# A diffusion backbone step: the block inverses of RWKV's pairs on four quarters of TensorE, in seven levels

## The reference, cut to what matters

```
def _rwkv_direction(r, w, k, v, a, b, s0):
    def step(state, inp):
        r_t, w_t, k_t, v_t, a_t, b_t = inp
        sa = jnp.einsum('bhvk,bhk->bhv', state, a_t)
        state = (state * w_t[:, :, None, :] + sa[..., None] * b_t[:, :, None, :]
                 + v_t[..., None] * k_t[:, :, None, :])
        return state, jnp.einsum('bhvk,bhk->bhv', state, r_t)
```

## Time and profile before

| | |
|---|---|
| timed runs, median | 2022.66 us |
| the profiled execution's own time | 2029.15 us |
| its span in the profile | 2027.2 us |
| mean granted TensorE clock | 0.96 |
| TensorE matmul busy | 1910.2 us (94%) |
| TensorE weight load busy | 1748.5 us (86%) |
| VectorE busy | 1095.8 us (54%) |
| ScalarE busy | 739.1 us (36%) |
| instructions | 38671 |

### The profile page before, as it was taken

The page is one execution under the profiler, slowest core; times in us unless marked ns, Lnnn a source line. Parts: engine busy times, 40 slices in busy tenths (PEclk is TensorE's granted clock), DMA queues, the critical chain, the costliest instruction groups (busy, mean ns, idle before and its releaser), DMA issues. The chain is left out here.

```text
span 2027.2 us, 38671 instructions
## 1 busy us (share of the span) xinstructions
PE 1910.2 (94%) x16360; PEld 1748.5 (86%) x16360; DVE 1095.8 (54%) x1845; ACT 739.1 (36%) x1108; POOL 33.2 (2%) x62
## 2 busy tenths in 40 slices
PE   5999999998888989999999999999978898999997
PEld 2888999995665879999999999999747497999997
DVE  3544444865537466554455554476564756655533
ACT  3333333435224244333343333344441424433322
POOL 0000000000001000000000000000000100000000
PEclk9999999998789999999999999999979798999999
DMA  7766233423446233333343333442240401333332
GB/s 271 263 224 222 90 129 137 158 101 113 142 129 212 85 109 125 124 124 113 127 145 124 124 118 114 138 169 90 87 148 4 159 13 66 125 124 124 105 128 89
DMA packets 73192, 263.25 MB, mean 130 GB/s; under 512 B 9696, under 2 KB 10848, under 8 KB 56928
## 3 DMA queue, kind: packets, MB, share of 16 engines
q1 hardware_dynamic: 73056, 261.27, 37.9%
HBM read 259.08 MB, written 2.16 MB: 129 GB/s over the span
## 5 line engine op out<-in xcount | busy, mean ns | idle before, releaser
L157 PE MATMUL ps<-h_head,w_head 128*128 128x386 f32 x1824 | 624.0, 342 | 9.2 <-DVEq L243 4.1
L157 PE MATMUL ps<-h_head,w_rest 128*128 128x386 f32 x1824 | 619.3, 340 | 0.0
L157 PE MATMUL ps<-h_rest,w_head 128*128 128x386 f32 x1824 | 617.3, 338 | 0.0
L219 ACT ACTIVATE w_head<-w_raw 128x2048 fp32r<-128x2048 f32 (+1 forms) x176 | 303.0, 1721 | 609.2 <-PE ps L157 598.9
L222 DVE TENSOR_TENSOR w_rest<-w_raw,w_head 128x2048 fp32r<-128x2048 f32 (+1 forms) x176 | 360.7, 2049 | 204.4 <-ACT w_head L219 204.3
L157 PEld LDWEIGHTS ps<-h_head,w_head 128*128 128x128 f32 x1824 | 345.9, 190 | 28.6 <-issue 18.8
L157 PEld LDWEIGHTS ps<-h_head,w_rest 128*128 128x128 f32 x1824 | 345.8, 190 | 0.0
L157 PEld LDWEIGHTS ps<-h_rest,w_head 128*128 128x128 f32 x1824 | 343.0, 188 | 0.2
L157 PE MATMUL ps<-gu_head,w_head 128*128 128x384 f32 x832 | 279.9, 336 | 11.4 <-DVE gu_rest L813 11.4
L157 PE MATMUL ps<-gu_rest,w_head 128*128 128x384 f32 x832 | 279.4, 336 | 0.0
L157 PE MATMUL ps<-gu_head,w_rest 128*128 128x384 f32 x832 | 279.3, 336 | 0.0
(11 more groups left out here) (294 smaller groups left out, 1798.1 us busy)
## 6 DMA issues: line engine op xcount, KB each, us to landing
w_raw<-in_w_in SPq DMA_DIRECT2D x88, 1024.0 KB, 4.8
w_raw<-in_w_out SPq DMA_DIRECT2D x64, 704.0 KB, 4.0
w_raw<-in_ada_w SPq DMA_DIRECT2D x41, 1024.0 KB, 6.2
ada_raw<-in_ada_w SPq DMA_DIRECT2D x31, 1024.0 KB, 6.4
w_raw<-in_mix_in SPq DMA_DIRECT2D x26, 1024.0 KB, 4.9
w_raw<-in_mix_out SPq DMA_DIRECT2D x8, 1024.0 KB, 5.0
hyena_const<-in_hconst SPq DMA_DIRECT2D x2, 1792.0 KB, 9.6
x<-in_x_in SPq DMA_DIRECT2D x1, 1536.0 KB, 12.2
```

The source lines that it names most:

```text
L157: return nc.tensor.matmul(out, lhsT, rhs, start=start, stop=stop)
L219: return nc.scalar.activation(self.HI[src], self.RAW[src], ACT.Copy)
```

## The change

The two directions now go through the inverse together. A new helper `crossed` issues the products of both: direction 0 on the two quarters as before, direction 1 with rows 0 to 63 of the array against columns 64 to 127 and the other way round, into a second PSUM bank. Direction 1's result therefore lands with its heads swapped, and the next product swaps them back. `straight` issues both directions on the old two quarters, where no swap is wanted (`pe_t`, `pe_y`). The first squares (`pe_s1`) keep the old two quarters too.

The running sums are replaced by products: T = I + D is multiplied by I + D^2 (`J2`), I + D^4 (`J4`) and I + D^8 (`J8`), and Y = (I + EX^2)(I + EX) Q. There are seven levels: `s1`; `d4`, `t1`, `x4`; `t2`, `x8`; `t`; `q`, `ex`; `gm`, `y1`, `ex2`; `y`. A pair issues 336 matmuls for its inverses, where it issued 288. Most copies out of PSUM now take both directions at once, 128x768 over two neighbouring banks; X^4 and EX are read twice by VectorE, once with the identity added and once plain.

The pairs share bank 3 in place of bank 6, since the two banks of a copy must be neighbours; GLA and pair B move to banks 4, 5, 6. B may write bank 3 when A's `y1` is copied. All four hand-written queues are reordered: the `ada_products` of the second set are issued during A's inverse, and in `two_pairs_stage` B's inverse is laced with A's recurrence.

```diff
--- before.py
+++ after.py
@@ -1340,13 +1340,12 @@
-                                " ".join(f"s{i}_{z}" for i in ("1", "2") for z in z2) + " s2q_0 s2q_1 s3_0 s3q_0 s3_1 s3q_1 " +
-                                " ".join(f"s{i}_{z}" for i in ("4", "5", "6", "7", "8", "9") for z in z2) + " " +
+                                "s1_0 s1_1 d4 t1 x4 t2 x8 t q ex gm y1 ex2 y " +
...
-                                " ".join(f"s{i}_{z}" for i in (1, 2, 3, 5, 6) for z in z2) + " u0 u1 u2 u3 o sq std")
+                                "d2_0 d2_1 d4 t1 t_0 q gm y1 y_1 u0 u1 u2 u3 o sq std")
...
-                                " ".join(f"s{i}_{z}" for i in ("1", "2q", "3q", "4", "7", "8", "9") for z in z2) + " " +
+                                "x2_0 x2_1 j2_0 j2_1 j4 x4 t2 j8 t_1 je ex jg y_0 " +
...
-                self.D, self.D2, self.D4, self.Y, self.ET = (by_chunk(b) for b in (self.SIG, self.E2, self.E3, self.CUM, self.E1))
-                self.GS, self.D8, self.EX = self.D4, self.D2, self.D
+                self.D, self.D2, self.J2, self.J4, self.ET = (by_chunk(b) for b in (self.SIG, self.E2, self.E3, self.CUM, self.E1))
+                self.X, self.T = (self.XQ[:, :, :, x, :] for x in range(2))
+                self.D4, self.X4, self.J8 = self.D, self.D2, self.X
+                self.INV, self.Q, self.EX, self.JE, self.G = self.J2, self.T, self.D, self.J4, self.X
+                self.Y1, self.JG, self.Y = self.D2, self.ET, self.J4
...
-            def each(self, b, lhsT, rhs):
-
-                for c, e in PROBS:
-                    last = mm(bank(b, TOK)[half(e), c * C:c * C + C], lhsT(c, e), rhs(c, e))
+            def crossed(self, ba, bb, lhsT, rhs):
+                for c in range(NCH):
+                    for h in range(2):
+                        mm(bank(ba, TOK)[half(h), c * C:c * C + C], lhsT[half(h), 0, c, :], rhs[half(h), 0, c, :])
+                    for h in range(2):
+                        last = mm(bank(bb, TOK)[half(1 - h), c * C:c * C + C], lhsT[half(h), 1, c, :], rhs[half(h), 1, c, :])
                 return last
...
+            def straight(self, ba, bb, lhsT, rhs):
+
+                for z, b in enumerate((ba, bb)):
+                    for c in range(NCH):
+                        for h in range(2):
+                            last = mm(bank(b, TOK)[half(h), c * C:c * C + C], lhsT[half(h), z, c, :], rhs[half(h), z, c, :])
+                return last
+
+            def even(self):
+                return (self.b0, self.b1) if self.b3 > self.b2 else (self.b1, self.b2)
+
+            def odd(self):
+                return (self.b2, self.b3) if self.b3 > self.b2 else (self.b3, self.b0)
+
+            def both(self, banks):
+                ba, bb = banks
+                assert bb == ba + 1
+                return PS[:, ba * 512:bb * 512 + 512].rearrange("p (z x) -> p z x", x=512)[:, :, 0:TOK].rearrange("p z (c t) -> p z c t", t=C)
+
+            def one_of(self, banks, z):
+                return bank(banks[z], TOK).rearrange("p (c t) -> p c t", t=C)
...
-            def pe_s2(self, pe, z):
-                ba, _ = self.pair_banks(z)
-                self.after_act(pe, f"s1_{z}")
-                self.after_dve(pe, f"s1_{z}")
-                self.pe_step(self.each(ba, self.power(z), self.of(self.D2, z)), f"s2_{z}")
...
-            def pe_s789(self, pe, i, z):
-                ba, _ = self.pair_banks(z)
-                if i == 7:
-                    self.after_act(pe, f"s6_{z}")
-                else:
-                    self.after_dve(pe, f"s{i - 1}_{z}")
-                self.pe_step(self.each(ba, self.of(self.EX, z), self.q(z) if i == 7 else self.of(self.Y, z)), f"s{i}_{z}")
+                ba, bb = self.even()[z], self.odd()[z]
+                for b, lhsT, rhs in ((ba, self.X, self.D), (bb, self.D, self.X)):
+                    for c in range(NCH):
+                        for h in range(2):
+                            last = mm(bank(b, TOK)[half(h), c * C:c * C + C], lhsT[half(h), z, c, :], rhs[half(h), z, c, :])
+                self.pe_step(last, f"s1_{z}")
+
+            def pe_d4(self, pe):
+                self.after_act(pe, "d2_1")
+                self.after_dve(pe, "x2_1")
+                self.pe_step(self.crossed(*self.even(), self.X, self.D2), "d4")
+
+            def pe_t1(self, pe):
+                self.after_dve(pe, "j2_1")
+                self.after_pool(pe, "q1")
+                self.pe_step(self.crossed(*self.odd(), self.J2, self.T), "t1")
+
+            def pe_x4(self, pe):
+                self.after_act(pe, "d4")
+                self.pe_step(self.crossed(*self.even(), self.D2, self.X), "x4")
+
+            def pe_t2(self, pe):
+                self.after_dve(pe, "j4")
+                self.after_act(pe, "t1")
+                self.pe_step(self.crossed(*self.odd(), self.J4, self.T), "t2")
+
+            def pe_x8(self, pe):
+                self.after_dve(pe, "x4")
+                self.pe_step(self.crossed(*self.even(), self.D4, self.X4), "x8")
+
+            def pe_t(self, pe):
+                self.after_dve(pe, "j8")
+                self.pe_step(self.straight(*self.odd(), self.J8, self.T), "t")
...
+            def pe_ex(self, pe):
+                self.after_act(pe, "t_0")
+                self.after_dve(pe, "t_1")
+                self.pe_step(self.crossed(*self.odd(), self.ET, self.INV), "ex")
+
+            def pe_g(self, pe):
+                self.after_act(pe, "q")
+                self.pe_step(self.crossed(*self.even(), self.INV, self.ET), "gm")
+
+            def pe_y1(self, pe):
+                self.after_act(pe, "q")
+                self.after_dve(pe, "ex")
+                self.pe_step(self.crossed(*self.odd(), self.JE, self.Q), "y1")
+
+            def pe_ex2(self, pe):
+                self.after_act(pe, "gm")
+                self.after_dve(pe, "ex")
+                self.pe_step(self.crossed(*self.even(), self.G, self.EX), "ex2")
+
+            def pe_y(self, pe):
+                self.after_dve(pe, "jg")
+                self.after_act(pe, "y1")
+                self.pe_step(self.straight(*self.even(), self.JG, self.Y1), "y")
 
             def pe_x(self, pe, t):
                 if t == 0:
-                    self.after_dve(pe, "s9_1")
+                    self.after_dve(pe, "y_0")
+                    self.after_act(pe, "y_1")
...
+            def act_both(self, act, name, out, banks):
+                self.after_pe(act, name)
+                self.act_step(nc.scalar.activation(out, self.both(banks), ACT.Copy), name)
+
+            def act_d4(self, act):
+                self.after_pool(act, "q1")
+                self.act_both(act, "d4", self.D4, self.even())
...
+            def dve_one_plus(self, dve, product, out, banks, name):
+                self.after_pe(dve, product)
+                ones = cst("istack").unsqueeze(1).unsqueeze(1).to_broadcast([128, 2, NCH, C])
+                self.tt(out, self.both(banks), ones, ALU.add, name)
+
+            def dve_one_plus_x4(self, dve):
+                self.dve_one_plus(dve, "x4", self.J4, self.even(), "j4")
+
+            def dve_x4(self, dve):
+                self.after_pe(dve, "x4")
+                self.dve_step(nc.vector.tensor_copy(self.X4, self.both(self.even())), "x4")
...
-                A = Pair(scope, SEMS[0:5], lay, 0, (0, 1, 2), 6, PR, TG, AL, MO)
-                G = Gla(scope, SEMS[5:10], lay, (3, 4, 5), P, MO)
+                A = Pair(scope, SEMS[0:5], lay, 0, (0, 1, 2), 3, PR, TG, AL, MO)
+                G = Gla(scope, SEMS[5:10], lay, (4, 5, 6), P, MO)
...
-                A = Pair(scope, SEMS[0:5], lay, 1, (0, 1, 2), 6, PR, TG, AL, MO)
-                B = Pair(scope, SEMS[5:10], lay, 2, (3, 4, 5), 6, PR, TG, AL, MO, (A.act_done, A.AC["s6_1"]))
+                A = Pair(scope, SEMS[0:5], lay, 1, (0, 1, 2), 3, PR, TG, AL, MO)
+                B = Pair(scope, SEMS[5:10], lay, 2, (4, 5, 6), 3, PR, TG, AL, MO, (A.act_done, A.AC["y1"]))
```

476 lines of the change are left out of this document (214 added, 262 removed).

## The result

The changed kernel takes 2045.1 us (median of 4 runs, 2041.07 to 2048.98) against 2022.84 us for the kernel before beside it. The ratio is 1.0102, 95% interval 1.0085 to 1.0118: about 1% slower, where 0.5% faster was forecast. The medians differ by 22.3 us.

A forecast was written before the change was run, and what follows sets the result against it. It took the inverse as bound by TensorE and the recurrence by round trips of x and u through VectorE. Four stage gains summed to -9.5 us off the median 2022.66: 2013 us, eight-in-ten range 2003 to 2030.

The forecast's parts named there:

- The question that it took for the risk: Crossed steps of the inverse: whether four quarters run side by side; 0.70 us for 24 matmuls, up to 1.40 without overlap.
- A crossed step takes 0.70 to 0.80 us.: Inverse, timeline after: the successor of a crossed step of 48 records starts 0.70 to 0.80 us later.
- the slower rival: Ten crossed steps of each inverse: four quarters are no faster than two, 1.40 us a step, 2042 us; 14%.
- GLA stage, second layer, -3.2: Second layer's GLA stage: inverse ends sooner, part is lost again before the second x; -3.2 us.
- GLA stage, first layer, -2.2: First layer's GLA stage: five `ada_products` cover most waits in the inverse, the second round loses that cover; -2.2 us.
- what else moves I cost at nothing: ... SP's loads only start sooner: Everything else that moves, including modulation weights, pool's T = I + D and SP's loads: priced at nothing.
- Two-pair stages, -3.3 and -0.8: Two-pair stages: A's first x comes much earlier and the stage ends sooner; -3.3 us first layer, -0.8 us second.
- A's norm is now out of the way and the end loses its doubled copies: Second layer's two-pair stage, after B's first x: a shorter end, last output at 69.4 us, before 70.2.
- The clock: Mixer stages: TensorE is busy 77% at a granted 1.00 in the recurrence, and no stretch much emptier was expected.
- The sign of a wrong mechanism: The four stages: the mechanism is wrong if their granted clock falls below that of the windows before.
- The sum: All four stages together: -3.2 - 2.2 - 0.8 - 3.3 = -9.5 us.

The follow-up runs named there:

- e1: Kernel before plus a block of crossed, straight and load-accompanied crossed steps that wait for nothing; a long-running crossed step took 1.37 us.
- e3: Changed kernel with every crossed step made straight (two quarters instead of four); ratio 1.0143 to the kernel before.
- e2: Changed kernel with the second sets' modulation weight loads cut to one eighth in the first layer; ratio 1.0029 to the kernel before.
- e13: Kernel before with its old inverse, but the second layer's two-pair stage in the changed kernel's order; ratio 1.0030, stage 76.5 us.
- e14: Kernel before with the new inverse in the second layer's two-pair stage, B on its own banks, both recurrences in step; ratio 1.0003, stage 69.3 us.
- e5: Kernel before with the change in the GLA stages of both layers only; ratio 1.0006.
- e6: Kernel before with the change in the two-pair stages of both layers only; ratio 1.0074.
- e9: Kernel before with the new inverse in the second layer's two-pair stage, B on its own banks, its recurrence one round behind; ratio 1.0039, stage 78.8 us.
- e7: Kernel before with the change in the GLA stages only, the second set's products left in their old places; ratio 1.0002.
- e12: Kernel before with the change in the second layer's GLA stage alone, a repeat with more rounds; ratio 0.9986.

## Why the prediction was wrong

The question that it took for the risk, whether four quarters overlap, was answered rightly. What decided the time, how fast instructions reach TensorE, was not in it, and the order that lets A go first was priced too low.

- *A crossed step takes 0.70 to 0.80 us.* Right in the trace (0.75), and the copies (0.81, 0.95) to the hundredth. But 0.70 us holds only while instructions lie ready. In the long run it is 1.37 us (e1). That the slower rival (2042 us) comes near the measured 2045.1 is luck: its cause, quarters that don't overlap, is refuted by the 0.75, and with steps that really take 1.40 us the kernel comes to 1.0143 (e3), some 2052 us. The trace's 48 records in 0.70 us are 15 ns each, where the Trainium skill's "TensorE: Matmul & The Clock Gate", section "Wait — 56ns, not 53.3ns?", has a floor of 25; over a whole stream they are 28.5 ns (3.65 us for 128).
- *GLA stage, second layer, -3.2.* Measured -3.1, but by two misses that cancel: A's x stands at 31.3 us instead of the 29.6 worked out (1.4 us of stops ahead of it), and behind the second x (38.0) the recurrence gained 1.0 us where I had given it nothing.
- *GLA stage, first layer, -2.2.* Measured +7.8. The step that failed is "what else moves I cost at nothing: ... SP's loads only start sooner". The loads, started sooner by the products in the inverse, fell on the instruction fetches, and a step priced at 0.70 us took its instructions faster than they came: 6.5 us of stops (2.3 are left in e2 without the loads), and some 3 us of half clock behind them (0.6 and 0.7 us in the two rows behind the stop at 555.88, 0.25 for `t`, 0.8 for `y` at 576.57, 0.6 for the two products behind it). Together 9.5 of the 10.0 us between forecast and result; e2's stage is 6.5 us shorter.
- *Two-pair stages, -3.3 and -0.8.* Measured +7.0 and +5.0. Stops are 5.7 and 2.0 of that. A's x came as worked out in the second layer (25.3 against 25.6), B's at 46.5 against 43.8. The step that failed is "A's norm is now out of the way and the end loses its doubled copies": from B's first x to the end of the last output I gave 25.6 us, it took 28.8, because B runs its round trips alone and the granted clock goes to 0.50, TensorE's 1.2 GHz. e13 prices the order at 6.9 us without any new level; in the changed kernel the levels gave about 2 of it back (74.7 against 76.5), and without the order they give nothing (e14). In the first layer A's x came at 32.2 instead of 27.9, and B's at 53.2, 7.9 us later than before (45.3), while the part from there on took 28.9 against 29.8: there the whole loss stands ahead of B's first x. I had counted what ends A's inverse sooner, and put B's delay against it too low.
- *The clock.* The sign of a wrong mechanism came: the granted clock fell in three of four stages (0.92, 0.89, 0.90 in the windows above). Their busy shares are 84, 79 and 78%, no lower than the 77% that I had gone by, so the share of a whole stretch did not tell it. The half clock stands behind the long stop and in the lone tail, where TensorE is busy for 5.75 of 11.70 us (726.33 to 738.03). The idle 3.71 us with a lower clock behind it stood in the earlier trace rows as a warning.
- *The sum.* GLA stages +4.7, two-pair stages +12.1, elsewhere +1.2 in the trace. e5 and e6 put the larger part on the two-pair stages too: 0.06% (-0.15 to 0.26) and 0.74% (0.52 to 0.96).

What could have been read before: TensorE's 863 matmul and 863 weight-load records in 31.31 us are 55 a us, and the change asks for 96 instructions in 0.70 us in its steps. That is a question to ask, though no row of before showed the limit. At the 70 a us of e1 or the 76 of e9, the 336 matmuls of a pair, 1344 instructions, take 18 to 19 us, an estimate: no less than the 18.1 us of the inverse before.

Stage times of single executions scatter: with the same stage code the second layer's two-pair stage took 74.7 and 76.0 us in two kernels and 77.3 in e2, with 2.0, 5.1 and 3.7 us of stops, and I can't say why e2's is longest. How much of the two-pair stages' loss is supply, and how much order, is therefore known to 2 or 3 us only. That a fetch waits behind the load's packets is inferred from the stops' lengths and the packets' starts with and without loads (e1, e2, e7); no record says what a packet waits for.

No version beat the kernel before measurably; the nearest is the new inverse in the second layer's GLA stage alone (0.9986, up to 1.0001).

## What to carry to other kernels

Before small matmuls are made faster, count instructions per microsecond. In these runs TensorE got 70 to 76 a us over a long stretch, and making a step faster than that mostly turned work into waiting. Fewer, wider matmuls would ask for fewer instructions; no run here tried them. Look at which bank or order a faster part forces on its neighbour; a chain that is put behind its neighbour starts late, and where it ends alone it pays with its round trips and with the clock. And a load that "only starts sooner" is a change with a price of its own.

## What was not expected of the hardware

- TensorE's instructions came in pieces of 256, at best one in 3.2 us (two packets of e12) and 3.65 us on average with nothing else on the DMA engines (e1); beside 1 MB loads 4 to 6 us. About 205 matmul records lay ready at the start of e1's block.
- Four quarters of 64x64 ran 48 records in 0.70 us, 15 ns each.
- Behind the stop of 3.97 us the granted clock was 0.50 from 556.6 to 560.0 us. Behind one of 1.08 us (575.21) it fell too, behind one of 1.97 us (686.98) it did not.
